# A three-layer float32 block on one core: weight chunks split whole, not in halves, from q, k to the gates

## The chip, the cores and the metric

The kernel runs on one core of a Trainium2 chip. The metric is the device time of one execution in microseconds, the median over several runs. TensorE multiplies matrices. ScalarE and VectorE do elementwise work, GpSimd (POOL) does a little of it, and SyncE (SP) starts the transfers. Each engine has its own queue of instructions, works it off in order, and waits for the others only at semaphores.

## The reference

The input is x with 256 tokens of 1024 channels, in float32. Three blocks follow, each with a norm before and after and a residual sum: a gated DeltaNet mixer, a short convolution mixer, and a third block, in which the change lies. Cut to what matters of it:

```
h = rmsnorm(x) * (1 + scale) + shift
q, k, v, z_ret, u_val, u_gate, z_conv, g_a, g_b = split(h @ w_in)
ret = head_groupnorm(retention_chunkwise(rotary(q), rotary(k), v))
y_a = (ret * silu(z_ret)) @ w_ret_out
a   = causal_depthwise_conv(u_val * sigmoid(u_gate))          # 31 taps
y_b = (silu(layernorm(a)) * silu(z_conv)) @ w_conv_out
y   = (sigmoid(g_a) * y_a + sigmoid(g_b) * y_b) @ w_out
x   = x + gate * rmsnorm(y)
```

## The kernel before

**Split products.** Every weight and every activation is cut into a high part in TensorE's rounded float32 format and a low part, the difference. A product is then hi x hi + hi x lo + lo x hi, three matmuls. For weights ScalarE copies `raw` to `w_hi` (`split_hi`, L1213), and VectorE subtracts: `w_lo = raw - w_hi` (`split_lo` through `part_lo`, L1777).

**Chunks and phases.** The weights pass in 128 chunks of 1 MB (128 partitions x 2048 elements), in the order of `PHASES`. The change touches `qk` (8 chunks), `v` (8), `zret` (8), `zconv` (4) and `gates` (8); `glu` stands before them and `ret_out` behind. SP brings each chunk to one of four slots of `raw` and may refill a slot when both low halves of its chunk are done (`lo_ready`).

**Halves.** A chunk is split in two halves of 128x1024. There are four tiles of high halves and four of low ones, so two chunks fit. In step c of a phase, while TensorE multiplies chunk c, ScalarE and VectorE each split the second half of chunk c+1 and the first half of chunk c+2 (`split_ahead`). Half h of a chunk waits, through `half_done`, until TensorE has done half h of the chunk two back.

**TensorE.** For each half it waits for `hi_ready`, does the products with the high weights, waits for `lo_ready`, and does those with the low weights. In qk and zconv the weights are the stationary operand (L676, L677, then L685); in v, zret and gates they are the moving one (L726, L727, then L733). Between chunks it does the retention's own products and transposes (L1127, L1139, L1141, L1153).

**What stands beside the splits.** The order on each engine is the order in which the code is written. Besides the splits VectorE has in step c: the rotation of q and k in qk (L2435 to L2439), the masks of the scores in v (L2449), statistics of the group norm in zret (L2456 to L2471), low parts of the turned result in zconv, and in every step a share of the 248 tap operations of the depthwise convolution (`conv_share`, L2389): 3 a step in qk, 8 or 9 in v, 7 in zret, 5 to 8 in zconv, and in gates 4, then 10 in each of the next five steps, then the last one. ScalarE evicts results (L1632, L1638, among them `vt`, `zr` and `gab`) and does the group norm (L1647, L1653). GpSimd multiplies group-normed results by their gates in zret and the first zconv step (L1764), and adds pairs for the layer norm in zconv.

Of the kernel before, what the change touches and what calls it, by code (L numbers as in the profile page):

```python
# [9 lines left out]
F32R = mybir.dt.float32r  # L10
I32 = mybir.dt.int32
ACT = mybir.ActivationFunctionType
# [4 lines left out]
P = 128  # L17
# [3 lines left out]
KT = D // P  # L21
KH2 = KT // 2
# [29 lines left out]
CC = 256  # L52
RING = 4
# [3 lines left out]
READ_BY = {name: "act" if name in ("z", "v", "zret", "zconv", "gates") else "dve" for name in ORDER}  # L57
DEEP = ("gdn_out", "sc_out", "ret_out")
DEEP_NEXT = ("sc_in", "glu")
CW2 = 2 * CC  # L60
OUT_PIECES = 2
END_BANKS = (3, 4)
# [2 lines left out]
COUNT = dict(PHASES)  # L65
# [33 lines left out]
def build(nc, x_in, pre_norm_w, post_norm_w, gdn_w_in, gdn_conv_w, gdn_A_log, gdn_dt_bias, gdn_norm_w, gdn_w_out,  # L99
# [3 lines left out]
    with ctx:  # L103
# [17 lines left out]
        def new(name, shape, dt=F32):  # L121
            n = 4
            for s in shape[1:]:
                n *= s
            return at(name, room(n), shape, dt)
# [1 line left out]
        K = 1024  # L127
        o_raw = top[0]
        raw = [new(f"w_raw{s}", [P, KT, CC]) for s in range(RING)]
        w_hi = [new(f"w_hi{s}", [P, KH2, CC], F32R) for s in range(4)]  # L130
        w_lo = [new(f"w_lo{s}", [P, KH2, CC], F32R) for s in range(4)]
        x = new("x", [P, NT, D])
        o_hT, o_yT, o_ada, o_ar = room(16 * K), room(32 * K), room(8 * K), room(64 * K)

# [87 lines left out]
        vt = at("vt", o_q + 16 * K, [P, NT, 2 * D])  # L222
# [25 lines left out]
        raw_ready = [sem(f"raw_ready{s}") for s in range(RING)]  # L248
        hi_ready, lo_ready = sem("hi_ready"), sem("lo_ready")
        half_done = sem("half_done")  # L250
# [94 lines left out]
        def half_slot(g, h):  # L345

            moved = FIRST["sc_in"] < g < FIRST["glu"]
            return (g + moved) % 2 * 2 + h

        def at_least(g0, i, j):  # L350

            return g0 + j + 4 * (i if isinstance(i, int) else 1)
# [849 lines left out]
        def _(act):  # L1202
            def split_hi(g0, i, j, h, home=None):

                if isinstance(i, int) and g0 + 4 * i + j >= CHUNKS:
                    return
                slot = j % RING
                if h == 0 and (g0, i, j) != (0, 0, 0):
                    act.wait_ge(raw_ready[slot], i * 16 + 16 * ((g0 + j) // RING + 1))
                g = at_least(g0, i, j)  # L1210
                sooner = {(1, 1): 3, (2, 0): 2, (2, 1): 2, (3, 0): -1}.get((g - FIRST["sc_in"] if g < FIRST["glu"] else g - FIRST["glu"], h), 0)
                act.wait_ge(half_done, i * 8 + (2 * (g0 + j) + h + 1 - sooner))
                act.activation(w_hi[half_slot(g, h if home is None else home)][:, :, :], raw[slot][:, h * KH2:(h + 1) * KH2, :], ACT.Copy).then_inc(hi_ready, 1)  # L1213

            def split_ahead(g0, i, j):
                split_hi(g0, i, j + 1, 1)
                split_hi(g0, i, j + 2, 0)
# [10 lines left out]
            def chunks(name, each=None, unroll=False, ahead=0, held=0, upto=None, sooner=None, apart=False):  # L1228

                g0 = FIRST[name]  # L1230

                def step(i):
                    for j in range(4 if upto is None else min(4, upto - 4 * i)):
                        if sooner is not None:
                            sooner(j)
                        if name in DEEP_NEXT and isinstance(i, int) and i == 0 and j < 2:
                            if j == 1:
                                split_hi(g0, i, j + 2, 0)
                        elif not unroll or ahead <= 4 * i + j < COUNT[name] - held:
                            split_ahead(g0, i, j)  # L1240
                        elif held and 4 * i + j == COUNT[name] - held:
                            split_hi(g0, i, j + 1, 1)
                            split_first_hi(ORDER[ORDER.index(name) + 1])
                        if j == 0 and name in HANDED and READ_BY[name] == "act":
                            act.wait_ge(bank_free, 4 + g0)
                        if each is not None:
                            each(i, j, i * 8 + (2 * (g0 + j) + 6))
                if unroll:
                    for i in range(COUNT[name] // 4):
                        step(i)  # L1250
                elif apart:
                    step(0)
                    with act.Fori(1, COUNT[name] // 4) as i:
                        step(i)
                else:
                    loop(act, COUNT[name] // 4, step)
# [366 lines left out]
                act.wait_ge(bank_free, i * 4 + (4 + g + j - 1))  # L1623
                act.activation(glu_part[j % 2][:, :, :], psum[:, 2 * j:2 * j + 2, SEQ:2 * SEQ], ACT.Copy).then_inc(sc_act, 1)
            chunks("glu", glu_each, apart=True)
            chunks("qk")

            def tokens_out(dst, func):
                def each(i, j, done):
                    if j % 2:  # L1630
                        act.wait_ge(half_done, done)
                        act.activation(dst[:, :, bass.ds(i * 1024 + j // 2 * CW2, CW2)], psum[:, j - 1:j + 1, :], func).then_inc(bank_free, 2)  # L1632
                return each

            def channels_out(dst, func):
# [1 line left out]
                    act.wait_ge(half_done, done)  # L1637
                    act.activation(dst[:, bass.ds(i * 8 + 2 * j, 2), :], bank(j), func).then_inc(bank_free, 1)  # L1638
                return each
            chunks("v", tokens_out(vt, ACT.Copy))  # L1640
            z_ret = tokens_out(zr, ACT.Silu)

            def group_norm(h):
# [32 lines left out]
            gates = tokens_out(gab, ACT.Sigmoid)  # L1676
# [98 lines left out]
        def _(dve):  # L1775
            def part_lo(o, whole, hi):
                return dve.tensor_tensor(o, whole, hi.bitcast(F32), ALU.subtract)  # L1777

            def split_lo(g0, i, j, h, home=None):

                if isinstance(i, int) and g0 + 4 * i + j >= CHUNKS:
                    return
                s = half_slot(at_least(g0, i, j), h if home is None else home)
                dve.wait_ge(hi_ready, i * 8 + (2 * (g0 + j) + h + 1))
                part_lo(w_lo[s][:, :, :], raw[j % RING][:, h * KH2:(h + 1) * KH2, :], w_hi[s][:, :, :]).then_inc(lo_ready, 1)

            def split_first_lo(name):
                g = FIRST[name]
                for h in range(2):
                    ks = slice(h * KH2, (h + 1) * KH2)  # L1790
                    n = DEEP_NEXT.index(name)
                    dve.wait_ge(hi_ready, 2 * g + h + 1)
                    part_lo(first_lo[n][:, ks, :], raw[g % RING][:, ks, :], first_hi[n][:, ks, :]).then_inc(lo_ready, 1)
                dve.wait_ge(hi_ready, 2 * g + 3)
                part_lo(second_lo[n][:, :, :], raw[(g + 1) % RING][:, 0:KH2, :], second_hi[n][:, :, :]).then_inc(lo_ready, 1)

            def chunks(name, each=None, unroll=False, before_last=None, ahead=0, held=0, upto=None, lead=None, sooner=None,
                       apart=False, between=None):
                g0 = FIRST[name]
                if lead is not None:  # L1800
                    lead()

                def step(i):
                    for j in range(4 if upto is None else min(4, upto - 4 * i)):
                        if sooner is not None:
                            sooner(j)
                        if name in DEEP_NEXT and isinstance(i, int) and i == 0 and j < 2:
                            if j == 1:
                                split_lo(g0, i, j + 2, 0)
                        elif not unroll or ahead <= 4 * i + j <= COUNT[name] - max(held, 1):  # L1810
                            split_lo(g0, i, j + 1, 1)
                            if between is not None:
                                between(i, j)
                            if not held or 4 * i + j < COUNT[name] - held:
                                split_lo(g0, i, j + 2, 0)
                            else:
                                split_first_lo(ORDER[ORDER.index(name) + 1])
                        if j == 0 and name in HANDED and READ_BY[name] == "dve":
                            dve.wait_ge(bank_free, 4 + g0)
                        if each is not None:  # L1820
                            each(i, j, i * 8 + (2 * (g0 + j) + 6))
                if unroll:
                    for i in range(COUNT[name] // 4):
                        step(i)
                elif apart:
                    step(0)
                    with dve.Fori(1, COUNT[name] // 4) as i:
                        step(i)
                elif before_last is not None:
                    loop(dve, COUNT[name] // 4 - 1, step)  # L1830
                    before_last()
                    step(COUNT[name] // 4 - 1)
                else:
                    loop(dve, COUNT[name] // 4, step)
# [792 lines left out]
```

## Time and profile before

| what | value |
|---|---|
| median of 3 runs | 839.99 us (839.98 to 840.67) |
| span of the profiled execution | 838.1 us |
| TensorE busy | 831.1 us (99%) |
| VectorE busy | 730.8 us (87%) |
| ScalarE busy | 500.2 us (60%) |
| mean granted TensorE clock | 0.998 of full speed |

The profile is of one execution. Its page gives the span, from the first to the last instruction, and no other time of that execution; the median of the runs is 1.9 us above this span. A busy share is an average over stages with different limits, so a stage is read from its own stretch of the timeline. On the timeline all times are us from the span's start. An entry in square brackets is the idle time of the engine before that instruction, with what ended it.

### The profile page before, as it was taken

The numbers are of one execution on the slowest core, as the hardware profiler recorded it, in microseconds if no ns is written. First come the engines' busy times: TensorE is split into PE (matmuls) and PEld (weight loads), VectorE is DVE, ScalarE is ACT, GpSimd is POOL, SyncE is SP. The second block draws the span as 40 slices with busy tenths as digits, with TensorE's granted clock in tenths as the row PEclk, the third lists the DMA queues.
The fourth block names the chain that finished last, engine by engine and source line by source line (L and its number), as shares of the span: only waits on it lengthen the run. The fifth ranks groups of instructions, "written<-read, shape, count | busy, mean of one in ns | idle before, by whom it ended". The sixth has DMA issues, their size and how long they took to land.

```text
span 838.1 us, 14189 instructions
## 1 busy us (share of the span) xinstructions
PE 831.1 (99%) x5274; PEld 733.4 (88%) x5274; DVE 730.8 (87%) x1179; ACT 500.2 (60%) x804; POOL 45.4 (5%) x46
## 2 busy tenths in 40 slices
PE   9999999999999999999999999999999999999997
PEld 8999998799889888888888898998887798888886
DVE  7799899867877988988979979999998999988774
ACT  6899858576556555554555674433346675546743
POOL 0001101341100000000000000000001220000000
PEclk9999999999999999999999999999999999999999
DMA  9875675601775787777775656655464436564531
GB/s 276 255 253 170 211 248 170 165 16 36 277 241 170 255 265 257 259 257 247 249 253 201 228 185 228 201 171 181 151 201 150 152 112 198 191 230 174 186 116 50
DMA packets 129883, 164.15 MB, mean 196 GB/s; under 512 B 17407, under 2 KB 92199, under 8 KB 129703
## 3 DMA queue, kind: packets, MB, share of 16 engines
q1 hardware_dynamic: 129831, 163.45, 59.6%
q8 instruction: 34, 0.56, 0.3%
q14 instruction: 18, 0.15, 0.1%
HBM read 159.20 MB, written 4.23 MB: 195 GB/s over the span
## 4 chain that ended last, share of the span: by engine, by line
PE 98%; DVE 1%; DMA 1%; ACT 0%; issue 0%; DVEq 0%; SPq 0%; ACTq 0%
PE psum L694 16%; PE psum L726 14%; PE psum L727 14%; PE psum L733 14%; PE psum L703 8%; PE psum L676 6%; PE psum L685 6%; PE psum L677 6%; PE psum L1023 3%; PE psum L629 1%; PE psum L640 1%; PE psum L633 1%; PE psum L914 1%; PE psum L1139 1%; PE psum L1127 1%; DMA x<-in_x_dram 1%
## 5 line engine op out<-in xcount | busy, mean ns | idle before, releaser
L1213 ACT ACTIVATE w_hi<-w_raw 128x1024 fp32r<-128x1024 f32 x257 | 268.5, 1060 | 187.3 <-PE psum L733 86.5
L1777 DVE TENSOR_TENSOR w_lo<-w_raw,w_hi 128x1024 fp32r<-128x1024 f32 x258 | 307.3, 1219 | 45.5 <-ACT w_hi L1213 43.5
L694 PE MATMUL psum<-hT,w_hi 128*128 128x512 f32 x576 | 138.9, 391 | 0.0
L694 PEld LDWEIGHTS psum<-hT,w_hi 128*128 128x128 f32 x576 | 105.3, 188 | 20.1
L726 PE MATMUL psum<-w_hi,hT 128*128 128x512 f32 x280 | 113.3, 405 | 0.0
L727 PE MATMUL psum<-w_hi,hT 128*128 128x512 f32 x280 | 109.3, 390 | 0.0
L2389 DVE SCALAR_TENSOR_TENSOR cv<-aP,par,cv 128x256 f32<-128x256 f32 x240 | 107.9, 518 | 0.0
L676 PE MATMUL psum<-hT,w_hi 128*128 128x256 f32 x432 | 107.4, 286 | 0.0
L677 PE MATMUL psum<-hT,w_hi 128*128 128x256 f32 x432 | 105.9, 283 | 0.0
L676 PEld LDWEIGHTS psum<-hT,w_hi 128*128 128x128 f32 x432 | 82.8, 192 | 0.4 <-issue 0.2
L677 PEld LDWEIGHTS psum<-hT,w_hi 128*128 128x128 f32 x432 | 82.8, 192 | 0.3 <-issue 0.2
L703 PEld LDWEIGHTS psum<-hT,w_lo 128*128 128x128 f32 x576 | 74.8, 191 | 3.3
L703 PE MATMUL psum<-hT,w_lo 128*128 128x256 f32 x576 | 76.1, 283 | 0.0
L726 PE MATMUL psum<-w_hi,yT_hi 128*128 128x512 f32 x192 | 75.7, 394 | 0.0
L733 PE MATMUL psum<-w_lo,hT 128*128 128x512 f32 x280 | 75.6, 390 | 0.0
L727 PE MATMUL psum<-w_hi,yT_lo 128*128 128x512 f32 x192 | 74.8, 390 | 0.0
L726 PEld LDWEIGHTS psum<-w_hi,hT 128*128 128x128 f32 x280 | 52.6, 188 | 12.0 <-issue 1.7
L727 PEld LDWEIGHTS psum<-w_hi,hT 128*128 128x128 f32 x280 | 52.6, 188 | 12.0 <-issue 1.7
L733 PEld LDWEIGHTS psum<-w_lo,hT 128*128 128x128 f32 x280 | 52.6, 188 | 11.2
L685 PE MATMUL psum<-hT,w_lo 128*128 128x256 f32 x432 | 60.6, 283 | 0.0
L685 PEld LDWEIGHTS psum<-hT,w_lo 128*128 128x128 f32 x432 | 55.7, 192 | 0.0
L733 PE MATMUL psum<-w_lo,yT_hi 128*128 128x512 f32 x192 | 52.7, 389 | 0.0
(353 smaller groups left out, 1138.5 us busy)
## 6 DMA issues: line engine op xcount, KB each, us to landing
w_raw<-in_w_in_dram SPq DMA_DIRECT2D x44, 1024.0 KB, 5.0
w_raw<-in_sc_w_in_dram SPq DMA_DIRECT2D x32, 1024.0 KB, 7.5
w_raw<-in_gdn_w_in_dram SPq DMA_DIRECT2D x23, 1024.0 KB, 7.4
ada<-in_w_ada_dram SPq DMA_DIRECT2D x24, 512.0 KB, 4.8
w_raw<-in_gdn_w_out_dram SPq DMA_DIRECT2D x8, 1024.0 KB, 5.3
w_raw<-in_sc_w_out_dram SPq DMA_DIRECT2D x8, 1024.0 KB, 5.3
w_raw<-in_w_ret_out_dram SPq DMA_DIRECT2D x8, 1024.0 KB, 5.0
w_raw<-in_w_conv_out_dram SPq DMA_DIRECT2D x4, 1024.0 KB, 5.2
```

What stands on the lines that cost most here:

```text
L676: pe.matmul(o[:, m, :], w_hi[s][:, k, mine], a_hi[:, ka, :], start=m == 0 and ka == 0, stop=False, skip_group_check=True)
L677: pe.matmul(o[:, m, :], w_hi[s][:, k, mine], a_lo[:, ka, :], start=False, stop=False, skip_group_check=True)
L685: mm = pe.matmul(o[:, m, :], w_lo[s][:, k, mine], a_hi[:, ka, :], start=False, stop=ka == KT - 1, skip_group_check=True)
L694: pe.matmul(o, w_hi[s][:, k, mine], hT[:, h * KH2 + k, :, :], start=h == 0 and k == 0, stop=False, skip_group_check=True)
L703: mm = pe.matmul(o, w_lo[s][:, k, mine], hT_hi[:, ka, :], start=False, stop=ka == KT - 1, skip_group_check=True)
L726: pe.matmul(psum[:, b + m, :], a_hi[:, ka, mine], wide(w_hi[s])[:, e, :], start=start and h == 0 and e == 0, stop=False, skip_group_check= ...
L727: pe.matmul(psum[:, b + m, :], a_lo[:, ka, mine], wide(w_hi[s])[:, e, :], start=False, stop=False, skip_group_check=True)
L733: mm = pe.matmul(psum[:, b + m, :], a_hi[:, k + 2 * h + e, mine], wide(w_lo[s])[:, e, :], start=False, stop=stop and h == 1 and e == 1, sk ...
L1023: mm = pe.matmul(b[:, a, :], left(a), right(a), start=True, stop=True)
L1213: act.activation(w_hi[half_slot(g, h if home is None else home)][:, :, :], raw[slot][:, h * KH2:(h + 1) * KH2, :], ACT.Copy).then_inc(hi_r ...
L1777: return dve.tensor_tensor(o, whole, hi.bitcast(F32), ALU.subtract)
L2389: dve.scalar_tensor_tensor(out=cv[:, n, :], in0=src, scalar=w, in1=cv[:, n, :], op0=ALU.mult, op1=ALU.add).then_inc(cv_step, 1)
```

## The change

In the five phases of `WHOLE` a step no longer makes two half splits. It makes one split of all 128x2048 elements of the next chunk: one copy on ScalarE (`split_hi_whole`) and one subtraction on VectorE (`split_lo_whole`). The four high tiles become two tiles of a whole chunk each, with the old names as views of their halves; the same for the low ones. The whole copy waits until both halves of the chunk two back are done, and the whole subtraction until the whole copy is. Each adds 2 to its semaphore, so TensorE's and SP's waits stay as they are. At the seams a half remains: in step 0 of qk the second half of chunk 1, and in the last step of gates, behind the whole chunk 0 of ret_out, the first half of its chunk 1. ScalarE's steps of qk and v are written out and no longer a loop.

```diff
+WHOLE = ('qk', 'v', 'zret', 'zconv', 'gates')
...
-        w_hi = [new(f"w_hi{s}", [P, KH2, CC], F32R) for s in range(4)]
-        w_lo = [new(f"w_lo{s}", [P, KH2, CC], F32R) for s in range(4)]
+        whole_hi, whole_lo = ([new(f"w_{n}{s}", [P, KT, CC], F32R) for s in range(2)] for n in ("hi", "lo"))
+        w_hi, w_lo = ([whole[s // 2][:, s % 2 * KH2:(s % 2 + 1) * KH2, :] for s in range(4)] for whole in (whole_hi, whole_lo))
...
+            def split_hi_whole(g0, i, j):
+                act.wait_ge(raw_ready[j % RING], i * 16 + 16 * ((g0 + j) // RING + 1))
+                act.wait_ge(half_done, i * 8 + (2 * (g0 + j) + 2))
+                act.activation(whole_hi[half_slot(at_least(g0, i, j), 0) // 2][:, :, :], raw[j % RING][:, :, :], ACT.Copy).then_inc(hi_ready, 2)
...
+                        elif name in WHOLE:
+                            if name == WHOLE[0] and isinstance(i, int) and i == 0 and j == 0:
+                                split_hi(g0, i, j + 1, 1)
+                            else:
+                                split_hi_whole(g0, i, j + 1)
+                            if name == WHOLE[-1] and 4 * i + j == COUNT[name] - 1:
                                 split_hi(g0, i, j + 2, 0)
...
-            chunks("qk")
+            chunks("qk", unroll=True)
...
-            chunks("v", tokens_out(vt, ACT.Copy))
+            chunks("v", tokens_out(vt, ACT.Copy), unroll=True)
...
+            def split_lo_whole(g0, i, j):
+                s = half_slot(at_least(g0, i, j), 0) // 2
+                dve.wait_ge(hi_ready, i * 8 + (2 * (g0 + j) + 2))
+                part_lo(whole_lo[s][:, :, :], raw[j % RING][:, :, :], whole_hi[s][:, :, :]).then_inc(lo_ready, 2)
```

VectorE's `chunks` gets the same branch with `split_lo` and `split_lo_whole`.

VectorE before, in gates, steps 3 to 6 (`w_lo` low halves, `w_raw` slots, `w_hi` high halves, `cv` the convolution's sum; the number behind a name tells its buffer):

```order
L1777 TENSOR_TENSOR w_lo_58<-w_raw_49,w_hi_54 128x1024 [waits hi_ready]
L1777 TENSOR_TENSOR w_lo_59<-w_raw_50,w_hi_55 128x1024 [waits hi_ready]
L2389 SCALAR_TENSOR_TENSOR cv<-aP,par,cv 128x256 [waits cv_step] x10
L1777 TENSOR_TENSOR w_lo_60<-w_raw_50,w_hi_56 128x1024 [waits hi_ready]
L1777 TENSOR_TENSOR w_lo_57<-w_raw_51,w_hi_53 128x1024 [waits hi_ready]
L2389 SCALAR_TENSOR_TENSOR cv<-aP,par,cv 128x256 [waits cv_step] x10
L1777 TENSOR_TENSOR w_lo_58<-w_raw_51,w_hi_54 128x1024 [waits hi_ready]
L1777 TENSOR_TENSOR w_lo_59<-w_raw_52,w_hi_55 128x1024 [waits hi_ready]
L2389 SCALAR_TENSOR_TENSOR cv<-aP,par,cv 128x256 [waits cv_step] x10
L1777 TENSOR_TENSOR w_lo_60<-w_raw_52,w_hi_56 128x1024 [waits hi_ready]
L1777 TENSOR_TENSOR w_lo_57<-w_raw_49,w_hi_53 128x1024 [waits hi_ready]
L2389 SCALAR_TENSOR_TENSOR cv<-aP,par,cv 128x256 [waits cv_step]
```

VectorE after, the same steps (the changed kernel's lines are numbered some 13 to 25 higher):

```order
L1790 TENSOR_TENSOR w_lo_55<-w_raw_49,w_hi_53 128x2048 [waits hi_ready]
L2414 SCALAR_TENSOR_TENSOR cv<-aP,par,cv 128x256 [waits cv_step] x10
L1790 TENSOR_TENSOR w_lo_56<-w_raw_50,w_hi_54 128x2048 [waits hi_ready]
L2414 SCALAR_TENSOR_TENSOR cv<-aP,par,cv 128x256 [waits cv_step] x10
L1790 TENSOR_TENSOR w_lo_55<-w_raw_51,w_hi_53 128x2048 [waits hi_ready]
L2414 SCALAR_TENSOR_TENSOR cv<-aP,par,cv 128x256 [waits cv_step] x10
L1790 TENSOR_TENSOR w_lo_56<-w_raw_52,w_hi_54 128x2048 [waits hi_ready]
L2414 SCALAR_TENSOR_TENSOR cv<-aP,par,cv 128x256 [waits cv_step]
```

Each pair of halves has become one whole subtraction. The second half of a pair was for the chunk after the next; this work now stands one step later, behind ten taps.

ScalarE before, in gates, steps 0 to 3 (`gab` is the eviction of two chunks of gate logits):

```order
L1213 ACTIVATE w_hi_56<-w_raw_50 128x1024 [waits half_done]
L1213 ACTIVATE w_hi_53<-w_raw_51 128x1024 [waits half_done,raw_ready2]
L1213 ACTIVATE w_hi_54<-w_raw_51 128x1024 [waits half_done]
L1213 ACTIVATE w_hi_55<-w_raw_52 128x1024 [waits half_done,raw_ready3]
L1632 ACT_TABLE_LOAD [waits half_done]
L1632 ACTIVATE gab<-psum 128x2x512
L1213 ACTIVATE w_hi_56<-w_raw_52 128x1024 [waits half_done]
L1213 ACTIVATE w_hi_53<-w_raw_49 128x1024 [waits half_done,raw_ready0]
L1213 ACTIVATE w_hi_54<-w_raw_49 128x1024 [waits half_done]
L1213 ACTIVATE w_hi_55<-w_raw_50 128x1024 [waits half_done,raw_ready1]
```

ScalarE after, the same steps:

```order
L1219 ACTIVATE w_hi_54<-w_raw_50 128x2048 [waits half_done,raw_ready1]
L1219 ACTIVATE w_hi_53<-w_raw_51 128x2048 [waits half_done,raw_ready2]
L1645 ACT_TABLE_LOAD [waits half_done]
L1645 ACTIVATE gab<-psum 128x2x512
L1219 ACTIVATE w_hi_54<-w_raw_52 128x2048 [waits half_done,raw_ready3]
L1219 ACTIVATE w_hi_53<-w_raw_49 128x2048 [waits half_done,raw_ready0]
```

The first eviction, with its table load, now stands before the whole copy for chunk 3, of which the first half before was made ahead of it.

## Rows read from the trace of the kernel before

The rows by stage hold: the stretch, its length, then busy time and count of TensorE, its weight loads, VectorE, ScalarE and GpSimd, the granted clock, the transfers' share, and GB/s.

**Rows 1.** The page: busy time of TensorE and VectorE, and the chain by engine.

```profile
PE 831.1 (99%) x5274; PEld 733.4 (88%) x5274; DVE 730.8 (87%) x1179; ACT 500.2 (60%) x804; POOL 45.4 (5%) x46
...
PE 98%; DVE 1%; DMA 1%; ACT 0%; issue 0%; DVEq 0%; SPq 0%; ACTq 0%
```

**Rows 2.** Busy time by stage: qk, gates, and all five.

```profile
523.60:569.70 46.10, 46.10 (x386) 46.10 (x385) 45.49 (x75) 17.45 (x17) 0.00 (x0) 1.00 0.57 184
...
699.30:742.90 43.60, 43.60 (x195) 36.09 (x194) 43.60 (x80) 21.72 (x22) 0.00 (x0) 1.00 0.54 170
sum 219.30, PE 219.30 PEld 190.07 DVE 214.33 ACT 111.78 POOL 14.26; mean PE 43.86 PEld 38.01 DVE 42.87 ACT 22.36 POOL 2.85
```

**Rows 3.** The page's groups of splits, and a weight chunk's transfer.

```profile
L1213 ACT ACTIVATE w_hi<-w_raw 128x1024 fp32r<-128x1024 f32 x257 | 268.5, 1060 | 187.3 <-PE psum L733 86.5
L1777 DVE TENSOR_TENSOR w_lo<-w_raw,w_hi 128x1024 fp32r<-128x1024 f32 x258 | 307.3, 1219 | 45.5 <-ACT w_hi L1213 43.5
...
w_raw<-in_w_in_dram SPq DMA_DIRECT2D x44, 1024.0 KB, 5.0
```

**Rows 4.** VectorE in gates by time: start, us, what, count.

```profile
715.09 2.35 DVE L1777 TENSOR_TENSOR w_lo<-w_raw,w_hi 128x1024 fp32r<-128x1024 f32 x2
717.36 4.04 DVE L2389 SCALAR_TENSOR_TENSOR cv<-aP,par,cv 128x256 f32<-128x256 f32 x10
721.32 2.36 DVE L1777 TENSOR_TENSOR w_lo<-w_raw,w_hi 128x1024 fp32r<-128x1024 f32 x2
...
740.01 2.37 DVE L1777 TENSOR_TENSOR w_lo<-w_raw,w_hi 128x1024 fp32r<-128x1024 f32 x2
```

**Rows 5.** TensorE in the last chunk of gates, by time.

```profile
737.44 0.39 PE L726 MATMUL psum<-w_hi,hT 128*128 128x512 f32 x1
...
739.25 1.07 PE L733 MATMUL psum<-w_lo,hT 128*128 128x512 f32 x4
...
741.97 1.07 PE L733 MATMUL psum<-w_lo,hT 128*128 128x512 f32 x4
```

**Rows 6.** 512 elements on VectorE, twice in a row, in qk.

```profile
531.16 0.68 DVE L2435 TENSOR_TENSOR rp<-psum,trig 128x512 f32<-128x512 f32 x1
531.76 0.68 DVE L2436 TENSOR_TENSOR rp<-psum,trig 128x512 f32<-128x512 f32 x1
```

**Rows 7.** ScalarE in v, zret, zconv and gates, by time.

```profile
609.03 1.05 ACT L1213 ACTIVATE w_hi<-w_raw 128x1024 fp32r<-128x1024 f32 x1
...
632.02 1.03 ACT L1632 ACTIVATE zr<-psum 128x1024 f32<-128x1024 f32 x1
632.94 1.05 ACT L1213 ACTIVATE w_hi<-w_raw 128x1024 fp32r<-128x1024 f32 x1
...
683.21 0.60 ACT L1638 ACTIVATE zc<-psum 128x512 f32<-128x512 f32 x1
...
712.70 1.05 ACT L1213 ACTIVATE w_hi<-w_raw 128x1024 fp32r<-128x1024 f32 x1
```

**Rows 8.** VectorE in zret and zconv, by time.

```profile
636.32 1.23 DVE L1777 TENSOR_TENSOR w_lo<-w_raw,w_hi 128x1024 fp32r<-128x1024 f32 x1 [1.07 <-ACT w_hi L1213]
637.93 0.17 DVE L2456 RECIPROCAL grs<-grs 128x2 f32<-128x2 f32 x1 [0.38 <-ACT grs L1647]
...
666.29 4.94 DVE L2389 SCALAR_TENSOR_TENSOR cv<-aP,par,cv 128x256 f32<-128x256 f32 x7
...
687.83 2.34 DVE L1777 TENSOR_TENSOR w_lo<-w_raw,w_hi 128x1024 fp32r<-128x1024 f32 x2
```

**Rows 9.** TensorE in v and zconv, by time.

```profile
615.07 1.07 PE L733 MATMUL psum<-w_lo,hT 128*128 128x512 f32 x4
...
686.01 0.36 PE L676 MATMUL psum<-hT,w_hi 128*128 128x256 f32 x1
...
688.00 1.12 PE L685 MATMUL psum<-hT,w_lo 128*128 128x256 f32 x8
```

**Rows 10.** GpSimd in zret, by time.

```profile
667.27 2.89 POOL L1764 TENSOR_TENSOR vt<-og,zr 128x512 f32<-128x512 f32 x2 [11.15 <-ACT og L1653]
```

More of the change, by code:

```diff
@@ L1237, in step @@
                             if j == 1:
+                                split_hi(g0, i, j + 2, 0)
+                        elif name in WHOLE:
[4 more added lines that the diff above has]
+                            if name == WHOLE[-1] and 4 * i + j == COUNT[name] - 1:
                                 split_hi(g0, i, j + 2, 0)
@@ L1808, in step @@
                             if j == 1:
+                                split_lo(g0, i, j + 2, 0)
+                        elif name in WHOLE:
+                            if name == WHOLE[0] and isinstance(i, int) and i == 0 and j == 0:
+                                split_lo(g0, i, j + 1, 1)
+                            else:
+                                split_lo_whole(g0, i, j + 1)
+                            if name == WHOLE[-1] and 4 * i + j == COUNT[name] - 1:
                                 split_lo(g0, i, j + 2, 0)
```

## The prediction

> **What bounds the kernel now.** The page's first section comes first: TensorE is busy for 831.1 of 838.1 us, and the chain that ended last is 98% TensorE [rows 1]. So nothing is won by making ScalarE or VectorE cheaper; the only question is whether weights still arrive before TensorE asks for them. The table by stage is next: over qk, v, zret, zconv and gates TensorE is busy for all of the 219.3 us, and VectorE for 214.3 [rows 2]. VectorE is nearly as full as TensorE, and in gates it is full. Then the two groups that the change rewrites: a half split costs 1.06 us on ScalarE and 1.22 us on VectorE [rows 3]. Last come the timelines of VectorE, ScalarE and TensorE around the two tightest places [rows 4, 5, 7, 8, 9], to see by how much each low part is early.
>
> In gates a chunk lasts 5.44 us on TensorE (the low products of its halves start at 739.25 and 741.97, 2.72 apart [rows 5]), and a step of VectorE with ten convolution taps lasts 721.32 - 715.09 = 6.23 us [rows 4]. VectorE loses 0.79 us a step and lives on its lead. At the end little is left: step 6 starts at 740.01, its first subtraction (second half of the last chunk) ends about 1.22 later at 741.23, and TensorE takes it at 741.97 [rows 4, 5]. The slack is 0.74 us.
>
> **The change, part by part.** There are 36 steps in the five phases. Before, they hold 72 half splits on each engine. Now they hold 35 whole ones and 2 halves (second half of the second qk chunk, first half of the second ret_out chunk), so ScalarE and VectorE each issue 35 instructions fewer. TensorE's instructions and SP's transfers stay as they are.
>
> *Price of a whole operation.* No row has 2048 elements. On VectorE 512 elements take 0.68 us and start 0.60 apart, 1024 take 1.219 [rows 6, 3], and a pair of halves occupies 717.36 - 715.09 = 2.27 us [rows 4]. The slope is 0.537 us per 512, so a whole one ends 1.219 + 2 x 0.537 = 2.29 us after its start. For its place in the queue there are two bounds: nothing saved, 2.27; the whole fixed part of one operation saved, 1.219 - 1.074 = 0.145, so 2.125. The starts (1.135 and 0.60) put the fixed part that isn't overlapped at 1.135 - 1.074 = 0.06, so I take 2.21. On ScalarE 512 take 0.60, 1024 from PSUM 1.03 and a half 1.06 [rows 3, 6, 7], so a whole one takes 1.06 + 2 x 0.43 = 1.92.
> The Trainium skill ("VectorE: DVE Perf Modes", section on the TRN2 errata) says that an operation pays a fixed cost once however long its tile is, and gives an fp32 tensor_tensor as (N+151)/0.96 ns. For 1024 that is 1224 ns, which the 1219 of the rows bears out, and for 2048 it is 2291. By the rule that the 151 cycles are saved in full (0.157 us a step) the result would be some 842.3; the starts in the rows say that most of them is already overlapped.
>
> *What is due earlier.* Before, a chunk's first half was split two chunks ahead and only its second half one ahead. Now both wait until the chunk two back is done. In gates the low part of the first half is due 739.25 - 737.44 = 1.81 us into a chunk and the second half's 4.53 us [rows 5]. The operation that bounds is therefore due 2.72 us sooner, and ends 1.07 us later after its start, 3.8 us of slack gone. Given back is what VectorE no longer carries: the one half that it was ahead (1.13) and the saving per step. 0.74 - 3.8 + 1.13 is about -1.9 before the savings: negative, so TensorE must wait. The exact sum needs the ledger of the queue, from the last place where VectorE waits for ScalarE.
>
> *First stall, zconv.* In zret's step 2 ScalarE comes out of the zr eviction and may start the next split at 632.94 [rows 7]; chunk 1 is done by then (its eviction has just run). The whole high part is done at 634.86, and VectorE starts at 634.9. It reaches the reciprocal at 634.9 + 2.21 = 637.1, where before it had the second half still to do at 636.32 and reached it at 637.93 [rows 8]: 0.8 us ahead. From there to the pair of zconv's step 1, at 687.83 [rows 8], VectorE does not wait before, and six pairs of splits lie between, each 0.06 cheaper. So the subtraction for zconv's chunk 2 starts at 687.83 - 0.8 - 0.4 = 686.6 and ends at 688.9. TensorE wants it at 688.00 [rows 9]. Stall: 0.9 us.
>
> *Second stall, gates.* All TensorE times are now 0.9 later. The high part of gates' chunk 3 stands behind the first gab eviction with its table load, so ScalarE starts it at 712.70 + 0.9 = 713.6 and ends at 715.5 [rows 7]. VectorE would be ready earlier: 715.09 less the 1.2 us gained up to zconv and 0.06 for each of five more pairs, plus 0.4 us for waiting on chunk 2's high part, about 714.0 [rows 4]. So it waits and starts at 715.55. Four steps follow with ten taps each, at 2.21 + 3.96 = 6.17 us (3.96 is 6.23 - 2.27), so the subtraction for the last chunk starts at 740.2 and ends at 742.5. Before, TensorE started that chunk's low products at 739.25 [rows 5]. The difference, 3.25 us, is the whole delay, the 0.9 included; the rest comes as stalls of 0.2, 0.7, 0.7 and 0.7 us at chunks 4 to 7. Behind chunk 7 the last tap is out and VectorE catches up.
>
> *Edits at nothing.* The qk phase: both parts are ready 1.92 + 2.29 = 4.2 us after ScalarE starts, which it may do as soon as the chunk two back is done. They may take a chunk (46.1 us for eight, 5.76 [rows 2]) and its first high products, some 1.9 (686.01 to 688.00 [rows 9]); cover over 3 us. The v phase is tighter where the vt eviction comes first: for chunk 7 the high part starts at 609.03, the low part is there at 609.03 + 1.92 + 2.29 = 613.25, and is due at 615.07 [rows 7, 9]; cover 1.8 us. The ring's slot comes free later in a step by about an operation, with a transfer of 5.0 us [rows 3] against three chunks of 5.44 or more. The unrolled loops of ScalarE and the renamed tiles cost nothing under ScalarE's idle time [rows 2].
>
> *Sum.* 838.1 + 3.25 = 841.35 us of span. The page gives the span alone; the median of the runs is 1.9 above it, and carrying that over gives 839.99 + 3.25 = 843.2 us. With the low price (2.125) the first stall is 0.4 and the same ledger ends at +2.4; with the high one (2.27) the first stall is 1.4 and it ends at +4.0. The likeliest case's own range is 842.4 to 844.0.
>
> **The rivals.**
> 1. *Not slower: VectorE's lead is enough.* For the time to stay within 0.2% (1.7 us, about what a measurement of this kernel can tell from no change) the last ledger must end 1.6 us sooner, so a step of gates at or below 5.8 instead of 6.17 us, or VectorE's start on chunk 3 no later than 714.0. For it: the ledger adds some twenty operations whose durations are taken as they were, and 1.6 us is little beside them. Against: two halves stream for 2.15 us by the slope alone, so no saving reaches 0.4 us a step, and ScalarE's table load stands before chunk 3. If the slack held everywhere the time would be 840.0, from the point on where the step is as short as TensorE's chunk and its lead covers the rest. A gain has no place to come from, since TensorE never waits in these phases [rows 2].
> 2. *More is lost, in zret and zconv.* A GpSimd multiply of 2.89 us stretches seven taps to 4.94 us, where ten take 4.04 in gates [rows 4, 8, 10], so 2.1 us are added to 2.85. These fall on taps before and, by the order, still do; if one falls on a whole subtraction, that one is 2.1 us late against about 2 us of cover in zret, and at zconv's chunk 2, where there is none, the delay passes on in full. One such hit in zconv makes the first stall 3 us, and the sum +5.3: 845.3. For it: zconv's first step already has two GpSimd operations. The Trainium skill ("SBUF — State Buffer", on the shared port pair) says that the pair is locked for a whole instruction, so a longer one holds GpSimd off longer; by that the hit is passed to GpSimd's multiplies, whose results are due several us later, and the sum stays.
> 3. *Only one of the stalls.* If VectorE is 0.9 us further ahead in zconv, the first stall is absent, chunk 3's split starts at 714.65, and the sum is +2.35: 842.3. It is the low end of my own range.
>
> **How the numbers follow.** The forecast (with rival 3 as its low end) gets 0.79, rival 2 gets 0.10, rival 1 gets 0.11. The range leaves out half of rival 2 and most of rival 1: 841.6 to 845.0. Slower by over 0.2% is above 841.7: forecast and rival 2, 0.89 less 0.02 for the low edge of the forecast, 0.87. Within 0.2%: rival 1 and that edge, 0.13, of which 0.01 is given to faster by over 0.2%, so 0.12 and 0.01.
>
> **What would show it.** Right: TensorE waits for w_lo of the subtraction line before its low products, once in zconv's chunk 2 and in gates' chunks 4 to 7, about 3 us in all, none in qk and v; a whole subtraction of 2.29 us and a whole copy of 1.92; VectorE with new waits for w_hi in v and a long one at gates' chunk 3; the stage table the same but zconv 0.9 and gates 2.3 us longer, and the stages behind unchanged. Wrong: no waits of TensorE in gates (rival 1), waits above 1.5 us in zconv or any in zret (rival 2), or a whole subtraction whose place in the queue is not between 2.1 and 2.3 us.

## The result, and the profile after

| | before | after |
|---|---|---|
| median of 5 runs, us | 839.98 (839.86 to 840.67) | 843.88 (843.56 to 845.18) |
| ratio of the runs | 1 | 1.0042 (95% interval 1.0032 to 1.0053) |
| span of the profiled execution, us | 838.1 | 843.4 |

The change made the kernel 3.9 us slower. The forecast was 843.2, with 841.6 to 845.0 as its range.

One thing first on how the two profiles compare. The profiled execution of after is the slowest of its five runs, 845.18 us; the others' spans lie 1 to 1.6 us lower. Lined up matmul by matmul, its TensorE is already 1.46 us behind when q and k begin, half of it (0.73 us) since 27 us after the start. The code is the same up to there, and other runs below stand between -0.3 and 2.1 us at that place. So a time T of after, taken as T - 1.46, is compared with the kernel before in the changed phases.

The page of after, busy time and chain, answers [rows 1]:

```profile
PE 833.3 (99%) x5274; PEld 733.3 (87%) x5274; DVE 729.2 (86%) x1144; ACT 493.5 (59%) x769; POOL 45.4 (5%) x46
...
PE 85%; DVE 10%; SPq 1%; DMA 1%; ACT 1%; issue 1%; DVEq 0%; ACTq 0%
```

Each elementwise engine has 35 instructions fewer and is busy for less, VectorE by 1.6 us, ScalarE by 6.7. Yet a tenth of the chain is now VectorE's. The stages show where the time went: qk, v, zret, zconv, gates, with windows moved by about what TensorE lags at each edge (to 0.2 us). The columns are as in [rows 2].

```profile
525.10:571.20 46.10, 46.10 (x387) 46.10 (x386) 44.84 (x68) 14.96 (x9) 0.00 (x0) 1.00 0.56 183
571.20:620.20 49.00, 49.00 (x227) 40.87 (x226) 45.75 (x78) 18.07 (x11) 0.00 (x0) 1.00 0.52 172
620.20:674.30 54.10, 54.10 (x218) 40.54 (x216) 52.17 (x85) 33.02 (x29) 8.67 (x6) 1.00 0.48 156
674.30:701.80 27.50, 26.59 (x224) 26.37 (x223) 27.43 (x40) 17.57 (x21) 5.59 (x4) 1.00 0.47 153
701.80:748.00 46.20, 44.84 (x195) 35.79 (x194) 44.16 (x73) 21.37 (x16) 0.00 (x0) 1.00 0.54 175
```

And zconv before:

```profile
672.80:699.30 26.50, 26.50 (x226) 26.44 (x224) 26.43 (x43) 18.38 (x25) 5.58 (x4) 1.00 0.48 159
```

The first three are as long as before. By these windows zconv is 1.0 us longer and gates 2.6 (43.6 before). Matching products give the exact lag, against 686.01 and 688.00 in [rows 9] and 741.97 in [rows 5]:

```profile
687.48 0.36 PE L677 MATMUL psum<-hT,w_hi 128*128 128x256 f32 x1
...
690.53 1.22 PE L686 MATMUL psum<-hT,w_lo 128*128 128x256 f32 x8 [0.91 <-DVE w_lo L1790]
...
747.23 1.07 PE L734 MATMUL psum<-w_lo,hT 128*128 128x512 f32 x4
```

The lag is 1.46 us up to zconv's chunk 2 (1.47 by these rounded times), 2.62 behind it and 5.26 from the last chunk of gates on. So it grows by 1.16 us in zconv and by 2.64 in gates, 3.80 in all, and by no more behind them.

What TensorE waits for, by its matmuls and by its weight loads (line, releaser, us in total, times, longest):

```profile
PE psum L734 <- DVE w_lo L1790: 1.2, 3, 0.4
PE psum L686 <- DVE w_lo L1790: 0.9, 1, 0.9
```

```profile
PEld psum L734 <- DVE w_lo L1790: 3.0, 4, 0.8
...
PEld psum L686 <- DVE w_lo L1790: 1.1, 1, 1.1
```

Neither row existed before. There is one wait in zconv (L686) and four in gates (L734), none in qk, v and zret. The matmuls' idle time is the smaller number: it counts from the recorded end of the product before, and such a record lasts 0.39 us where the next product starts 0.23 us later. What a wait costs is read from the lag. In the window of these phases neither ScalarE nor VectorE has a wait for a transfer. The last stall answers the second low row of [rows 5]; 739.25 has become 744.34, and the four products behind a stall last 1.21 instead of 1.07 us:

```profile
741.07 1.07 PE L734 MATMUL psum<-w_lo,hT 128*128 128x512 f32 x4
744.34 1.21 PE L734 MATMUL psum<-w_lo,hT 128*128 128x512 f32 x4 [0.38 <-DVE w_lo L1790]
```

The two operations that the prediction had to price, from the groups of after by shape:

```profile
L1790 DVE TENSOR_TENSOR w_lo<-w_raw,w_hi 128x2048 fp32r<-128x2048 f32 x35 | 80.0, 2286 | 7.4 <-ACT w_hi L1219 6.6
L1219 ACT ACTIVATE w_hi<-w_raw 128x2048 fp32r<-128x2048 f32 x35 | 67.0, 1914 | 58.9 <-PE psum L686 31.2 <-PE psum L734 27.7
```

2.29 us on VectorE and 1.91 on ScalarE. The place in the queue is read where nothing waits, VectorE in gates (answers [rows 4]):

```profile
709.73 2.29 DVE L1790 TENSOR_TENSOR w_lo<-w_raw,w_hi 128x2048 fp32r<-128x2048 f32 x1 [0.69 <-ACT w_hi L1219]
711.94 4.05 DVE L2414 SCALAR_TENSOR_TENSOR cv<-aP,par,cv 128x256 f32<-128x256 f32 x10
717.34 2.29 DVE L1790 TENSOR_TENSOR w_lo<-w_raw,w_hi 128x2048 fp32r<-128x2048 f32 x1 [1.35 <-ACT w_hi L1219]
...
723.50 2.29 DVE L1790 TENSOR_TENSOR w_lo<-w_raw,w_hi 128x2048 fp32r<-128x2048 f32 x1
```

The taps start 2.21 us after the subtraction (709.73 to 711.94), and the step without a wait is 723.50 - 717.34 = 6.16 us. And here is the chain of after in order of time, at its two turns: start, length, what.

```profile
633.48 1.03 ACT zr L1645
634.51 1.81 ACT w_hi L1219
636.41 2.29 DVE w_lo L1790
...
687.00 1.27 DVE yT_lo L1790 x2
688.27 2.21 DVE w_lo L1790
690.53 1.22 PE psum L686 x8
...
714.40 1.03 ACT gab L1645
715.43 1.81 ACT w_hi L1219
...
717.34 2.29 DVE w_lo L1790
...
742.08 2.21 DVE w_lo L1790
...
744.34 1.21 PE psum L734 x4
```

Read it backwards. The stall at 744.34 hangs on VectorE without a gap down to 717.34, there on ScalarE's whole copy, and that on the eviction of `gab`, which had to wait for TensorE. The stall at 690.53 hangs on VectorE down to 636.41, there on the copy behind the eviction of `zr`.

### The profile page after: what moved, and what is told of

Read it like the earlier page. It is cut to its first block, busy times and chain, and to the rows that moved or that the text cites. A ratio compares the mean times of both kernels' runs of the same rounds, so it can differ in the third digit from the quotient of the medians.

```text
span 843.4 us, 14112 instructions
## 1 busy us (share of the span) xinstructions
PE 833.3 (99%) x5274; PEld 733.3 (87%) x5274; DVE 729.2 (86%) x1144; ACT 493.5 (59%) x769; POOL 45.4 (5%) x46
## 4 chain that ended last, share of the span: by engine, by line
PE 85%; DVE 10%; SPq 1%; DMA 1%; ACT 1%; issue 1%; DVEq 0%; ACTq 0%
PE psum L695 16%; PE psum L734 11%; PE psum L727 11%; PE psum L728 11%; PE psum L704 8%; PE psum L686 5%; PE psum L677 5%; PE psum L678 5%; DVE cv L2414 5%; DVE w_lo L1790 4%; PE psum L1024 3%; DMA w_raw<-in_gdn_w_in_dram 1%; PE psum L630 1%; PE psum L641 1%; PE psum L634 1%
## 5 line engine op out<-in xcount | busy, mean ns | idle before, releaser
L1790 DVE TENSOR_TENSOR w_lo<-w_raw,w_hi 128x1024 fp32r<-128x1024 f32 (+1 forms) x223 | 304.3, 1388 | 51.4 <-ACT w_hi L1214 42.3
L1214 ACT ACTIVATE w_hi<-w_raw 128x1024 fp32r<-128x1024 f32 x187 | 194.8, 1061 | 109.5 <-PE psum L734 41.5
L1219 ACT ACTIVATE w_hi<-w_raw 128x2048 fp32r<-128x2048 f32 x35 | 67.0, 1914 | 58.9 <-PE psum L686 31.2
L734 PE MATMUL psum<-w_lo,hT 128*128 128x512 f32 x280 | 76.2, 392 | 1.4 <-DVE w_lo L1790 1.2
L734 PEld LDWEIGHTS psum<-w_lo,hT 128*128 128x128 f32 x280 | 52.3, 188 | 14.0 <-DVE w_lo L1790 3.0
L686 PE MATMUL psum<-hT,w_lo 128*128 128x256 f32 x432 | 60.7, 283 | 0.9 <-DVE w_lo L1790 0.9
L686 PEld LDWEIGHTS psum<-hT,w_lo 128*128 128x128 f32 x432 | 55.7, 192 | 1.1 <-DVE w_lo L1790 1.1
```

Source lines behind the costliest of these rows:

```text
L686: mm = pe.matmul(o[:, m, :], w_lo[s][:, k, mine], a_hi[:, ka, :], start=False, stop=ka == KT - 1, skip_group_check=True)
L734: mm = pe.matmul(psum[:, b + m, :], a_hi[:, k + 2 * h + e, mine], wide(w_lo[s])[:, e, :], start=False, stop=stop and h == 1 and e == 1, sk ...
L1219: act.activation(whole_hi[half_slot(at_least(g0, i, j), 0) // 2][:, :, :], raw[j % RING][:, :, :], ACT.Copy).then_inc(hi_ready, 2)
```

## The experiments

The theory: the loss is lead. VectorE's low parts come later by the order (a chunk's first half is no longer split two chunks ahead) and by the length of the operation, and where VectorE's cover runs out, TensorE waits. The rivals: each rewritten step costs something; the written-out loops of ScalarE cost something; only the length counts; only the order counts; in gates VectorE's own backlog sets the stalls, not ScalarE's copy. "Difference" is between the medians of the kernel and of the kernel before on the same chip.

**Which phases.** Three runs with another tuple, nothing else:

```diff
-WHOLE = ('qk', 'v', 'zret', 'zconv', 'gates')
+WHOLE = ('gates',)                          # e1
+WHOLE = ('qk', 'v', 'zret', 'zconv')        # e2
+WHOLE = ('qk', 'v', 'zret')                 # e3
```

> Whole splits in gates alone (8 steps), halves everywhere before. Lead theory: TensorE has no wait in zconv (that stall was 1.0 us) and the gates stalls stay, because VectorE starts on chunk 3 when ScalarE is past the gab eviction: 714.75 + 4 x 6.16 + 2.29 = 741.7 against 739.25, and 0.2 us to restart TensorE, so +2.6 us, 842.6. Rival (a cost per rewritten step, 3.9 us over 35): +0.9 us, 840.9. Rival (the delay is in zconv and passed on): 840.0.

Measured: 842.82 against 840.58 us, +2.2 (ratio 1.0027, 1.0017 to 1.0037). Expected were +2.6, and in its trace TensorE's lag grows by 2.59 us, all of it in gates.

> Whole splits in qk, v, zret and zconv (28 steps), halves in gates. Lead theory: the zconv stall alone, about +1.1 us, 841.1, TensorE waiting once for w_lo at zconv's chunk 2; in gates none, since VectorE arrives there about 1.2 us ahead of its old place. Rival (cost per step): +3.0 us, 843.0.

Measured: 842.04 against 840.58, +1.5 (1.0018, 1.0008 to 1.0027). Its trace has the zconv wait alone, and TensorE's lag grows by 1.16 us there and nowhere else in these phases:

```profile
PEld psum L686 <- DVE w_lo L1790: 1.1, 1, 1.1
```

> Whole splits in qk, v and zret (24 steps), halves in zconv and gates. Lead theory: +0.0 us, 840.0; the cover of 1.8 to 3 us in these phases holds and TensorE has no new wait. Rival (cost per step, or the unrolled loops of ScalarE): +2.7 us, 842.7.

Measured: 840.63 against 840.58, +0.05 (1.0002, 0.9992 to 1.0011), with no wait for `w_lo`. So 24 of the 35 rewritten steps cost nothing, the other two phases cost 2.2 and 1.5, and their sum of 3.7 is close to the whole (by the traces 2.59 + 1.16 = 3.75 of 3.80). A cost per step is out.

**The unrolled loops.**

```diff
-            chunks("qk")
+            chunks("qk", unroll=True)
...
-            chunks("v", tokens_out(vt, ACT.Copy))
+            chunks("v", tokens_out(vt, ACT.Copy), unroll=True)
```

> The kernel before with ScalarE's loops of qk and v written out, nothing else. Lead theory: 840.0, no change. Rival (part of the 3.9 us is code that has to be fetched, or its place): 840.5 to 841.5.

Measured: 840.66 against 840.34, +0.3 (1.0008, 0.9999 to 1.0017). The interval reaches from nothing to 1.4 us, so the medians alone don't settle it. The traces do: its TensorE runs within 0.1 us of the kernel before from start to end, and the run above, which contains the same unrolling, is at +0.05.

**Order and length apart.** First the whole copy with the subtraction in two halves at its place, then halves on both engines in the new order:

```diff
 # e5, VectorE only
-                part_lo(whole_lo[s][:, :, :], raw[j % RING][:, :, :], whole_hi[s][:, :, :]).then_inc(lo_ready, 2)
+                for h in range(2):
+                    ks = slice(h * KH2, (h + 1) * KH2)
+                    part_lo(whole_lo[s][:, ks, :], raw[j % RING][:, ks, :], whole_hi[s][:, ks, :]).then_inc(lo_ready, 1)
 # e6: the same with a wait for each half, and on ScalarE
...
-                act.activation(whole_hi[half_slot(at_least(g0, i, j), 0) // 2][:, :, :], raw[j % RING][:, :, :], ACT.Copy).then_inc(hi_ready, 2)
+                for h in range(2):
+                    act.wait_ge(half_done, i * 8 + (2 * (g0 + j) + h + 1))
+                    act.activation(whole_hi[s][:, ks, :], raw[j % RING][:, ks, :], ACT.Copy).then_inc(hi_ready, 1)
```

> As the change, with the whole copy on ScalarE, but VectorE subtracts in two halves at the place of the whole one, each freeing TensorE by itself. Lead theory with both parts (order and length): the first half's low part is ready 1.07 us sooner, but a pair takes 2.27 instead of 2.20: zconv stall 0.3 us, gates 715.1 + 4 x 6.23 + 1.22 = 741.2 against 739.25, so +2.2 us with the restart, 842.2. Rival (only the length of the subtraction matters): 840.0. Rival (only the order matters, the length nothing): 843.9.

Measured: 842.47 against 840.34, +2.1 (1.0024, 1.0013 to 1.0034); the lag in its trace grows by 2.12 us, 0.39 in zconv and 1.73 in gates.

> Halves on both engines, but in the change's order: in a step both halves of the next chunk, none of the one after it. Each half waits for its own half two chunks back. Lead theory: no stall in zconv (first low half there at 687.8, due 688.0); in gates 714.0 + 4 x 6.23 + 1.22 = 740.1 against 739.25, +1.0 us, 841.0: the order costs about 1 us and the length the rest. Rival (only the length matters): 840.0. Rival (only the order matters): 843.9.

Measured: 841.29 against 840.34, +0.95 (1.0014, 1.0004 to 1.0023); the lag grows by 0.91 us, in gates alone. Both are where the ledger put them, and the rivals at 840.0 and 843.9 are out for both. In e6 the last chunk of gates shows the same race, lost by less: the first low half starts on VectorE at 739.32, and TensorE takes it when it ends.

```profile
739.32 2.35 DVE L1793 TENSOR_TENSOR w_lo<-w_raw,w_hi 128x1024 fp32r<-128x1024 f32 x2
```

```profile
740.60 1.21 PE L734 MATMUL psum<-w_lo,hT 128*128 128x512 f32 x4 [0.50 <-DVE w_lo L1793]
```

So of the 3.8 us of the traces the order takes 0.9, the whole copy another 1.2, and the whole subtraction the last 1.7 (by the medians 1.0, 1.2 and 1.8). These are the shares when the parts are added in this order; another order wasn't run.

**What sets the gates stalls.** The change with ScalarE's table load moved into idle time, and the change itself on the same chip:

```diff
-            gates = tokens_out(gab, ACT.Sigmoid)
+            gates_out = tokens_out(gab, ACT.Sigmoid)
+
+            def gates(i, j, done):
+                if i == 0 and j == 0:
+                    act.activation(warm[:, 0:1], eps_r[:, :], ACT.Sigmoid)
+                gates_out(i, j, done)
```

> The change, and in step 0 of gates one Sigmoid of a single column on ScalarE, so that the table of 1.28 us is loaded in its idle time and not before the first gab eviction. Lead theory: VectorE's chain in gates starts where ScalarE's copy for chunk 3 ends; VectorE waits 1.35 us there, so the whole chain moves 1.28 us earlier and the loss falls from 3.9 to 2.6 us: 842.6; the zconv stall stays. Rival (VectorE's own backlog sets the gates stalls): 843.9, no change.

Measured: 843.16 us, +3.0 over 840.18 (1.0032, 1.002 to 1.0045).

> The changed kernel once more, on the same chip as the run with the early table: 843.9, or +3.6 to +4.0 us over the kernel before, with the trace's delay in zconv and gates again 3.7 us and whatever the profiled run loses in other stages free to differ.

Measured: 844.67, +4.5 over 840.18 (1.0047, 1.0033 to 1.006). That is above the +3.6 to +4.0 that was expected, though the interval holds the first measurement's +3.9. Between the two runs lie 1.5 us, expected 1.3. The five executions of this run alone spread over 1.4 us, so the traces decide again. In the changed phases the lag grows by 2.46 us with the early table and by 3.75 without it, 1.29 less, for a table load of 1.28. VectorE of the run with the early table no longer waits on chunk 3's high part:

```profile
711.93 4.05 DVE L2419 SCALAR_TENSOR_TENSOR cv<-aP,par,cv 128x256 f32<-128x256 f32 x10
716.05 2.29 DVE L1795 TENSOR_TENSOR w_lo<-w_raw,w_hi 128x2048 fp32r<-128x2048 f32 x1
...
722.22 2.29 DVE L1795 TENSOR_TENSOR w_lo<-w_raw,w_hi 128x2048 fp32r<-128x2048 f32 x1
```

The copy was on the chain; the step of 6.17 us stays. With the table loaded early the taps end at 715.98 and the subtraction starts at 716.05, so now VectorE's own backlog sets its start. The rival names what comes next, only 0.1 us behind the copy.

**Is a whole operation itself harmful?** The change with the same taps dealt otherwise, so that VectorE works where it waited and has a shorter step in gates; then the same deal in the kernel before:

```diff
-                conv_share(9 if c < RH else 8)
+                conv_share((9, 10, 9, 11, 9, 10, 8, 8)[c])
...
-                conv_share(7)
+                conv_share(10 if n == 1 else 7)
...
-                conv_share(5 if j else 8)
+                conv_share(5)
...
-                conv_share(10 if c else 4)
+                conv_share((5, 13, 8, 8, 8, 8, 8, 8)[c])
```

> Whole splits as in the change, but the convolution's taps are dealt otherwise: v 9,10,9,11,9,10,8,8, zret 7 with 10 in step 1, zconv 5 each, gates 5,13,8,8,8,8 and the one left. So VectorE does taps where it waited for w_hi, and its step in gates is 2.20 + 8 x 0.396 = 5.37 us, below TensorE's 5.44. Lead theory: no wait of TensorE for w_lo, 840.0 (839.7 to 840.4). Rival (the whole operation itself costs, wherever it stands): 843 to 844.

Measured: 840.50 against 840.58, -0.1 us (0.9998, 0.9989 to 1.0007). TensorE has no wait for `w_lo` at all, and VectorE's step is 5.37 us:

```profile
716.83 2.29 DVE L1790 TENSOR_TENSOR w_lo<-w_raw,w_hi 128x2048 fp32r<-128x2048 f32 x1 [0.16 <-ACT w_hi L1219]
719.04 3.25 DVE L2414 SCALAR_TENSOR_TENSOR cv<-aP,par,cv 128x256 f32<-128x256 f32 x8
722.20 2.29 DVE L1790 TENSOR_TENSOR w_lo<-w_raw,w_hi 128x2048 fp32r<-128x2048 f32 x1
```

> The kernel before (half splits in the old order) with the taps dealt as in the run with taps moved. All theories: 840.0, since TensorE has no wait in these phases to lose; it shows whether moving taps by itself brings or costs anything.

Measured: 840.16 against 840.34, -0.2 (0.9995, 0.9985 to 1.0004). All 35 whole operations can stand in the kernel for nothing, if the taps give way; and no version was measurably faster than the kernel before, which fits TensorE having no idle time in these phases to give back [rows 2].

## Why the prediction was right

**The bound.** "Whether weights still arrive before TensorE asks for them" was the right question. VectorE and ScalarE were made cheaper, and the time rose.

**The price.** The whole subtraction was put at 2.29 us and is 2.286; its place at 2.21 and is 2.20 to 2.21 in gates; the whole copy at 1.92 and is 1.914; the step of gates at 6.17 and is 6.16. The Trainium skill ("VectorE: DVE Perf Modes", section on the TRN2 errata) has the duration right, 2291 ns against 2286. By an estimate from that page its 151 cycles are 0.157 us. What the queue saves is less: 0.06 us an operation, as the rows of before had said.

**The first stall.** Predicted: the subtraction for zconv's chunk 2 starts at 686.6 and TensorE waits 0.9 us. Measured: 688.20 - 1.46 = 686.74, low products 1.07 us late (690.53 - 1.46 - 688.00), and 1.16 us behind them. The place and the cause are right; the size is 0.26 us too small: 0.1 in VectorE's start, 0.05 from VectorE's end to TensorE's start, and 0.1 in the eight products behind the stall.

**The second stall.** Predicted: VectorE starts on chunk 3 at 715.55 after a wait, the last subtraction ends at 742.5, the delay is 3.25 us in all. Measured: 717.34 - 1.46 = 715.88 after a wait of 1.35, an end of 744.28 - 1.46 = 742.82, and 3.80 us. The steps held (24.65 us for four, put at 24.68), and so did ScalarE's start after the eviction: 712.70 plus a lag of 1.16 is 713.86, and 715.32 - 1.46 is the same. What is missing are small terms that the ledger left out or had too small. 0.26 came with the first stall. 0.08 lay between the copy's end and VectorE's start (0.11 where 0.03 was put), 0.06 between VectorE's end and TensorE's start, and 0.17 in the products behind the last stall. With them the forecast would have been 843.8. One reading was off without effect: VectorE without ScalarE's copy would have been ready at about 714.5, not 714.0, since it waited 0.69 us for chunk 2's high part where 0.4 was put.

**Edits at nothing.** qk, v and zret cost nothing, alone (+0.05) and in the whole. The cover of 1.8 us for v's chunk 7 is there: its subtraction ends at 612.47 + 2.29 = 614.76, and TensorE takes it at 616.53.

**The rivals.** Rival 1, lead enough, is out by four new waits in gates. Rival 2, more than 845 through GpSimd, did not come: zret has no wait and zconv's is 1.1. Its condition never arose. GpSimd's multiplies fell on taps again (seven taps 4.94 us), and every whole subtraction of zret and zconv took 2.27 to 2.29 us. Which engine would give way if they met isn't shown here. Rival 3, only one stall, is what the run with gates alone makes: +2.2 by the medians and 2.59 by the trace, where it had +2.35.

**What is left open.** The medians differ by up to 0.7 us from what the traces give for the changed phases (+4.5 against 3.75 in the second measurement of the change). Seven of the eleven profiled executions behind the change and the experiments come to q and k 0.6 to 2.1 us late, most of it lost around 27 us and 170 us from the start, with the early table at 438 us; the other four are within 0.3 us. All six kernels with whole steps or the new order in all five phases are among the seven. It isn't a fixed cost of theirs: two of the first five executions of after had a span of 841.8, only 3.7 us over the 838.1 of before. Whether such a loss falls more often on some kernels than on others wasn't tested.

## What to carry to other kernels

Where one engine is 99% busy and never waits for its suppliers, as here, merging instructions on the suppliers leaves nothing to win, and it can slow the kernel down: the merged result is due with its first part and ready with its last. Price such a change not by busy time but by a ledger of the supplier's queue: from the last place where it waits for someone, operation by operation, to the moment the result is due. If the ledger comes out negative, look for other work in the same queue that has no due time; here ten taps a step in gates became eight, with the rest moved to where VectorE waited, and the cost was gone.

## What was not expected of the hardware

A stall of TensorE costs a little more than the wait: the four low products behind it last 1.19 to 1.21 us instead of 1.07, eight narrow ones 1.22 instead of 1.12, at a granted clock of 1.00 in both stages. And stages that a change doesn't touch moved by up to 2.1 us between profiled executions (TensorE's lag where q and k begin was 2.1 us with taps moved, -0.07 with only the loops unrolled), more than some of the effects measured here, so single spans should be compared stage by stage.
